# A two-layer decoder trunk: one row of the first half moved ahead of the second half's mean and root, and the second half's first rows grouped one by one

## What is computed

```python
def _layernorm(x, g, b):
    mu = xf.mean(-1, keepdims=True)
    var = jnp.mean(jnp.square(xf - mu), -1, keepdims=True)
    return (xf - mu) * lax.rsqrt(var + LN_EPS) * g + b
...
    x = _layernorm(DEEPNORM_ALPHA * x + m, p['ln_mix_g'][layer], p['ln_mix_b'][layer])
    f, nb = _conv_ffn(x, buf_ffn[layer], ...)
    x = _layernorm(DEEPNORM_ALPHA * x + f, p['ln_ffn_g'][layer], p['ln_ffn_b'][layer])
```

## Time and profile before

| | us |
|---|---|
| median of 3 runs | 1442.95 |
| lowest, highest | 1442.28, 1443.3 |
| the profiled execution | 1441.92 |
| its span in the profile | 1440.1 |
| busy: PE | 1409.3 (98%) |
| busy: DVE | 835.6 (58%) |
| busy: ACT | 617.8 (43%) |
| busy: POOL | 72.6 (5%) |

### The profile page before, as it was taken

The page is one execution under the profiler, slowest core; times in us unless marked ns, Lnnn a source line. Parts: engine busy times, 40 slices in busy tenths (PEclk is TensorE's granted clock), DMA queues, the critical chain, the costliest instruction groups (busy, mean ns, idle before and its releaser), DMA issues.

```text
span 1440.1 us, 24539 instructions
## 1 busy us (share of the span) xinstructions
PE 1409.3 (98%) x10256; PEld 1382.1 (96%) x10256; DVE 835.6 (58%) x1265; ACT 617.8 (43%) x1009; POOL 72.6 (5%) x96
## 2 busy tenths in 40 slices
PE   7999999999999999999999999999999999999995
PEld 7999999999899999999999999999999999999995
DVE  6656665656755645433555778787555445345555
ACT  5444435444644144312433676746541343133434
POOL 0000101000400000000000310003000000000000
PEclk9999999999999999999999999999999999999998
DMA  8141322324132322222222122221223222222222
GB/s 281 49 121 59 96 72 77 101 87 163 43 103 70 93 76 85 79 84 77 85 80 83 59 74 69 78 74 60 90 72 103 74 89 87 90 74 81 82 74 82
DMA packets 37231, 125.18 MB, mean 87 GB/s; under 512 B 4352, under 2 KB 6528, under 8 KB 36864
## 3 DMA queue, kind: packets, MB, share of 16 engines
q1 hardware_dynamic: 34128, 113.78, 24.8%
q0 software_dynamic: 2560, 8.91, 2.2%
q10 hardware_dynamic: 432, 0.91, 0.2%
HBM read 115.96 MB, written 7.63 MB: 86 GB/s over the span
## 4 chain that ended last, share of the span: by engine, by line
PE 93%; DVE 3%; ACT 2%; issue 1%; DMA 0%; POOL 0%; POOLq 0%; DVEq 0%; SPq 0%; ACTq 0%
PE PS L596 29%; PE PS L597 28%; PE PS L598 28%; PE PS L756 1%; PE PS L848 1%; PE PS L765 1%; PE PS L771 1%; PE PS L715 1%; PE PS L736 1%; DVE Y L1510 1%; PE PS L745 0%; DVE Y L1522 0%; PE PS L749 0%; ACT Y L1021 0%; DMA raw<-weights 0%
## 5 line engine op out<-in xcount | busy, mean ns | idle before, releaser
L596 PE MATMUL PS<-xhi,whi 128*128 128x296 f32 (+1 forms) x2176 | 660.8, 304 | 14.1 <-DVE wlo L1247 7.8
L597 PE MATMUL PS<-xlo,whi 128*128 128x296 f32 (+1 forms) x2176 | 649.6, 299 | 0.0
L598 PE MATMUL PS<-xhi,wlo 128*128 128x296 f32 (+1 forms) x2176 | 647.8, 298 | 0.0
L596 PEld LDWEIGHTS PS<-xhi,whi 128*128 128x128 f32 x2176 | 411.2, 189 | 20.5 <-issue 8.7
L597 PEld LDWEIGHTS PS<-xlo,whi 128*128 128x128 f32 x2176 | 411.5, 189 | 1.4
L598 PEld LDWEIGHTS PS<-xhi,wlo 128*128 128x128 f32 x2176 | 410.2, 189 | 0.0
L596 PE MATMUL PS<-hhi,whi 128*128 128x296 f32 (+2 forms) x912 | 272.4, 299 | 0.4 <-DVE Y L1459 0.4
L597 PE MATMUL PS<-hlo,whi 128*128 128x296 f32 (+2 forms) x912 | 271.2, 297 | 0.0
L598 PE MATMUL PS<-hhi,wlo 128*128 128x296 f32 (+2 forms) x912 | 270.5, 297 | 0.0
L1240 DVE TENSOR_TENSOR wlo<-raw,whi 128x1024 fp32r<-128x1024 f32 (+1 forms) x195 | 235.2, 1208 | 45.1 <-ACT whi L882 40.6
L882 ACT ACTIVATE whi<-raw 128x1024 fp32r<-128x1024 f32 (+1 forms) x195 | 203.0, 1043 | 131.3 <-DMA raw<-weights 63.8
(11 more groups left out here) (227 smaller groups left out, 1215.7 us busy)
## 6 DMA issues: line engine op xcount, KB each, us to landing
raw<-weights SPq DMA_DIRECT2D x182, 512.0 KB, 3.5
raw<-weights SPq DMA_DIRECT2D x16, 384.0 KB, 3.0
Y<-xT SPq DMA_DIRECT2D x8, 296.0 KB, 4.5
yT<-Y SPq DMA_DIRECT2D x16, 144.0 KB, 1.8
C<-consts SPq DMA_DIRECT2D x1, 2146.5 KB, 9.2
S<-s_hgrn POOLq DMA_DIRECT2D x4, 512.0 KB, 4.6
S<-s_ret POOLq DMA_DIRECT2D x4, 512.0 KB, 6.0
hgrn_out<-S POOLq DMA_DIRECT2D x4, 512.0 KB, 5.4
```

The source lines that it names most:

```text
L596: pe.matmul(dst, wh, h, start=first, stop=False)
L597: pe.matmul(dst, wh, lo, start=False, stop=False)
L598: return pe.matmul(dst, wl, h, start=False, stop=last)
```

## The change

Two things are changed. ScalarE does `shifted(0, 5)`, which is row 7 of the first half, ahead of `mean(1)` and `root(1)` instead of behind them, in all four norms. And the second half's rows are grouped as the first half's were: rows 1 and 2 each by themselves instead of as a pair, on VectorE and ScalarE.

```diff
-NORM_ROWS = [[(0, 1), (1, 1), (2, 1), (3, 2), (5, 2), (7, 1)], [(0, 1), (1, 2), (3, 2), (5, 2), (7, 1)]]
+NORM_ROWS = [[(0, 1), (1, 1), (2, 1), (3, 2), (5, 2), (7, 1)], [(0, 1), (1, 1), (2, 1), (3, 2), (5, 2), (7, 1)]]
...
                 shifted(0, 4)
+                shifted(0, 5)
                 mean(1)
                 root(1)
-                shifted(0, 5)
                 for i in range(len(NORM_ROWS[1])):
                     shifted(1, i)
```

## The result

The changed kernel takes 1447.06 us (median of 7 runs, 1446.29 to 1447.58), against 1442.95 us of the kernel before (7 runs, 1441.99 to 1443.35). The ratio is 1.003, with a 95% interval of 1.002 to 1.004: 4.1 us slower. The prediction said 1447.5 us.

The account below looks back on a forecast made before the run. TensorE bounds the kernel; its third tile hangs on the second half's row 5, through VectorE's unbroken chain on the root. 3 x 1.12 + 1.15 = 4.51 us, so 1442.95 + 4.5 = 1447.5 us, range 1445.5 to 1448.6.

Parts of the forecast that it names:

- The gain that was expected to be worth nothing: Norms 0 to 2, half 0: TensorE's 1.27 us wait before step 7 goes, but returns as second-half waits.
- The price of the late root: Norms 0 to 2: ScalarE's L1004 and what hangs on it come 0.94 us later in each.
- The finer groups: Second half, norms 0 to 2: splitting rows 1 and 2 lengthens VectorE's chain by 0.18 us in each.
- Norm 3: End of the kernel: row 7 ahead of L1004 costs 0.66 us, the split 0.49, together 1.15.
- The sum: Whole kernel: 3.36 us from norms 0 to 2 plus 1.15 at the end, 4.51 us slower.
- The statement that nothing behind the norm takes the delay up: Behind step 5 of half 1, norms 0 to 2: the 1.12 us delay reaches the third tile whole.
- the gain was not kept: Rival, norms 0 to 2: second-half rows come in time, each norm gives 1.38 us; 1440.0 us, chance 0.07.
- the absorbed root: Rival, norms 0 to 2: something else holds row 5, so only splits cost there; 1444.6 us, chance 0.13.

Follow-up runs that it names:

- the move alone: Kernel before, with row 7 of the first half ahead of mean and root, rows 1 and 2 still a pair; 1446.66 us against 1442.80.
- The shorter chain: Kernel before, with VectorE's L1510 of the second half's rows 1 and 2 done while it waits for the root; 1440.36 us against 1442.48.

## Why the prediction was right

**The gain that was expected to be worth nothing.** The step said that the 1.27 us before step 7 would go whole and come back as waits of the second half. It did: counted as there, 0.83 for row 0, where I had worked out 0.8, and 1.29 for row 3, where I had said about 1.2. For row 2 only 0.12 came. From the last product of step 6 (385.50) to the third tile it is 12.46 us, where I had said 12.5. That such a wait is worth nothing was argued there; it is shown, for the kernel before, by the row 7 that came earlier with the root unmoved, which gained 0.0 us.

**The price of the late root**, 0.94, was 0.91 in norm 0 of the move alone (28.08 - 27.17). The pitch of 0.94 is that of row 7's two instructions in the kernel before; behind the pair of rows 5 and 6 they take 0.91.

**The finer groups**, 0.18, measured 0.19. By the fixed part that the Trainium skill gives (VectorE: DVE Perf Modes, the section on the errata, 120 cycles) the estimate was 0.125; the trace decides for 0.19. The prediction took the sum to be 0.2 us smaller by this estimate, which counts norms 0 to 2 only: in norm 3, where two instructions are split, it would have been 0.25 against the measured 0.50, and the whole 0.4 smaller. The rule of the Trainium skill that breaking up instructions may let work be completed sooner (Perfetto Trace Analysis, Optimizing Scalar/DVE Operations) has the condition that VectorE is not saturated, and in this stretch VectorE has no idle time. Moving its work into a wait gained there, where cutting it lost.

**Norm 3**, 0.66 + 0.49 = 1.15, measured 0.67 alone, 0.50 alone, and 1.15 together.

**The sum** of 4.51 stands against 4.54 from the trace (from the first L803 to the last rows) and 4.1 from the medians, whose spread of about 1 us covers the rest. The statement that nothing behind the norm takes the delay up held too: the wait at the third tile is 0.50 with the change and 0.49 without it.

**The rivals.** The move alone refutes both: with it norm 0 grew by 0.91 us, so the gain was not kept and the late root was not absorbed. The doubt behind the absorbed root was that another row might be the true limit where TensorE's lead is used up only at row 5. The trace of the kernel before speaks against that more clearly than I had read it:

```profile
390.40 0.30 PE L598 MATMUL PS<-xhi,wlo 128*128 128x296 f32 x1
390.71 0.40 PE L596 MATMUL PS<-xhi,whi 128*128 128x296 f32 x1
```

This is step 3 of half 1. It starts 0.31 us behind the product before instead of 0.137, so TensorE waited for row 3 already, too short for the view of waits to list, and the lead was used up there. The shorter chain shows that the doubt had a small point all the same, since TensorE's own products are the next limit, 0.57 us behind.

## What to carry to other kernels

The longest wait of the engine that bounds a kernel is not yet time to be gained. Ask what the engine will wait for next once that wait is gone, and whether this one hangs on what is moved to the back: here an engine with a steady supply of rows slower than their use came next, and everything that made its start late cost one to one. The answer holds for one state of the kernel: once the supply was made faster, the same wait in half 0 set the end of the norm. Where the supply chain has no idle time behind some start, two edits pay, an earlier start and work taken out of the chain into the wait before it, and smaller pieces cost their fixed part each.

## What the runs showed of the hardware

In the profiled execution of the move alone TensorE's granted clock fell once. This is the view by stretches, norm 2, then norm 0 and norm 1; the 3 us of each norm are taken at the same place, against the product that waits for row 1; the columns are the busy time and count of PE, PEld, DVE, ACT and POOL, the granted clock, the DMA share and GB/s:

```profile
1006.00:1009.00 3.00, 1.24 (x9) 0.87 (x7) 2.83 (x6) 2.62 (x5) 1.66 (x3) 1.00 0.00 0
1009.00:1012.50 3.50, 3.50 (x15) 3.50 (x16) 2.52 (x7) 3.30 (x7) 2.84 (x4) 0.52 0.00 0
...
387.22:390.22 3.00, 1.23 (x9) 0.85 (x7) 2.83 (x6) 2.62 (x5) 1.65 (x3) 1.00 0.00 0
...
826.62:829.62 3.00, 1.23 (x9) 0.85 (x7) 2.83 (x6) 2.62 (x5) 1.65 (x3) 1.00 0.01 3
```

In norm 2, behind the two waits of 0.69 and 1.07 us, the clock was granted at 0.52 for 3.5 us, which is the lower of its two levels, 1.2 GHz, and products started every 0.24 us instead of every 0.13. Norm 2 took 28.73 us (988.14 to 1016.87), 1.92 more than before, where norms 0 and 1 grew by 0.91 and 0.90; so the fall cost about 1 us. In norms 0 and 1 of the same execution TensorE had been busy 1.23 us of 3 at the same place, practically the 1.24 of norm 2, behind waits of the same length, and the clock stayed. So what TensorE did just before doesn't tell the norm with the fall from the two without it. It is one occurrence in one profiled execution; two of the seven executions of this kernel had a mean clock of 0.994, all the others of it 0.995 or 0.996, and those two (one of them the profiled one) took 1447.01 and 1447.09 us, the longest of the seven. That the two long waits have a part in it was not tested. It was not foreseen in the prediction, and the changed kernel's own profile, with a granted clock of 1.00 in the stretches of norms 0 and 2, doesn't show it.
